# Last norm on token rows with the residual added by TensorE, other skipped splits, and the root spread inside a unit

## What is computed

```python
def layer_norm(x, g, b):
    xf = x.astype(jnp.float32)
    mu = xf.mean(-1, keepdims=True)
    var = jnp.mean(jnp.square(xf - mu), -1, keepdims=True)
    return ((xf - mu) * lax.rsqrt(var + LN_EPS) * g.astype(jnp.float32) + b.astype(jnp.float32)).astype(x.dtype)
```

## Time and profile before

| | before |
|---|---|
| median of 3 runs | 928.47 us (927.08 to 929.01) |
| the profiled execution | 931.21 us |
| its span | 929.4 us |
| TensorE matmul busy | 895.8 us |
| VectorE busy | 679.0 us |
| ScalarE busy | 505.5 us |
| GpSimd busy | 125.5 us |
| granted TensorE clock, mean | 0.99 of full |
| read from HBM | 153.97 MB |

### The profile page before, as it was taken

How to read it: one execution, slowest core, us unless ns; L and a number is a source line. 1 busy time by engine, 2 the same in 40 slices (tenths; PEclk the granted TensorE clock), 3 DMA queues, 4 the chain that set the end, 5 groups by cost and what they waited for, 6 DMA issues and landing times.

```text
span 929.4 us, 18682 instructions
## 1 busy us (share of the span) xinstructions
PE 895.8 (96%) x7034; PEld 859.4 (92%) x7034; DVE 679.0 (73%) x1123; ACT 505.5 (54%) x753; POOL 125.5 (13%) x80
## 2 busy tenths in 40 slices
PE   6999799999999999999999999999999899999995
PEld 5977799999999999899999999999889899999995
DVE  5976787777777847778766776878676776667667
ACT  6345644433435556876555555564486654455453
POOL 1000000000000023001232310301210122223011
PEclk9999999999999999999999999999999999999998
DMA  8953275556553654336555555532324255556531
GB/s 306 334 205 100 90 226 182 180 181 198 179 188 121 220 185 159 133 114 219 184 173 192 168 193 182 182 114 92 113 93 162 82 187 181 180 181 191 177 106 46
DMA packets 44004, 155.71 MB, mean 168 GB/s; under 512 B 5066, under 2 KB 5557, under 8 KB 43957
## 3 DMA queue, kind: packets, MB, share of 16 engines
q1 hardware_dynamic: 42192, 151.12, 49.2%
q10 hardware_dynamic: 1317, 2.35, 0.7%
q0 software_dynamic: 448, 1.59, 0.6%
HBM read 153.97 MB, written 1.06 MB: 167 GB/s over the span
## 4 chain that ended last, share of the span: by engine, by line
PE 86%; DVE 5%; ACT 4%; issue 3%; POOL 1%; DMA 1%; SPq 0%; POOLq 0%; ACTq 0%; DVEq 0%
PE ps L394 21%; PE ps L395 21%; PE ps L396 21%; PE ps L438 3%; PE ps L440 3%; PE ps L439 3%; PE ps L411 1%; PE ps L418 1%; PE ps L412 1%; DVE w_lo L1277 1%; PE ps L483 1%; PE ps L485 1%; PE ps L484 1%; PE ps L501 1%; PE ps L764 1%
## 5 line engine op out<-in xcount | busy, mean ns | idle before, releaser
L394 PE MATMUL ps<-op_hi,w_hi 128*128 128x258 f32 (+1 forms) x1372 | 390.3, 284 | 0.9 <-DVE op_lo L1406 0.9
L396 PE MATMUL ps<-op_hi,w_lo 128*128 128x258 f32 (+1 forms) x1372 | 387.6, 283 | 0.0
L395 PE MATMUL ps<-op_lo,w_hi 128*128 128x258 f32 (+1 forms) x1372 | 387.4, 282 | 0.0
L1277 DVE TENSOR_TENSOR w_lo<-raw,w_hi 128x1024 fp32r<-128x1024 f32 x224 | 283.0, 1282 | 28.9 <-ACT w_hi L928 27.5
L928 ACT ACTIVATE w_hi<-raw 128x1024 fp32r<-128x1024 f32 x224 | 231.4, 1051 | 62.8 <-PE ps L396 30.6
L394 PEld LDWEIGHTS ps<-op_hi,w_hi 128*128 128x128 f32 x1372 | 260.1, 190 | 3.7 <-issue 1.6
L395 PEld LDWEIGHTS ps<-op_lo,w_hi 128*128 128x128 f32 x1372 | 260.9, 190 | 1.1
L396 PEld LDWEIGHTS ps<-op_hi,w_lo 128*128 128x128 f32 x1372 | 260.0, 189 | 0.0
L394 PE MATMUL ps<-mix_hi,w_hi 128*128 128x256 f32 x480 | 137.7, 287 | 2.5 <-DVE w_lo L1274 2.3
L396 PE MATMUL ps<-mix_hi,w_lo 128*128 128x256 f32 x480 | 135.7, 283 | 0.0
L395 PE MATMUL ps<-mix_lo,w_hi 128*128 128x256 f32 x480 | 135.7, 283 | 0.0
(11 more groups left out here) (251 smaller groups left out, 1091.2 us busy)
## 6 DMA issues: line engine op xcount, KB each, us to landing
raw<-in_stream SPq DMA_DIRECT2D x284, 512.0 KB, 3.4
x<-in_x SPq DMA_DIRECT2D x4, 256.0 KB, 5.6
bias<-bias_rows POOLq DMA_DIRECT2D x1, 1024.0 KB, 7.9
result<-x SPq DMA_DIRECT2D x4, 256.0 KB, 2.4
spans<-in_spans ACTq DMA_DIRECT2D x1, 576.0 KB
bias<-bias_rows POOLq DMA_DIRECT2D x1, 512.0 KB, 11.2
proj<-in_gmask ACTq DMA_DIRECT2D x1, 512.0 KB
masks<-in_masks ACTq DMA_DIRECT2D x1, 384.0 KB
```

The source lines that it names most:

```text
L394: pe.matmul(o, wh, xh, start=start, stop=False, **kw)
L395: pe.matmul(o, wh, xl, start=False, stop=False, **kw)
L396: return pe.matmul(o, wl, xh, start=False, stop=stop, **kw)
L1277: m = dve.tensor_tensor(w_lo[:, s, :], raw[:, s, :], fp(w_hi[:, s, :]), ALU.subtract)
```

## The change

1. In all feed-forwards, TensorE does the spread of the root after half of its third unit (`out_chunk` with `half`), not behind the unit. On VectorE only one split is left between the statistic and the copy of the root; the second stands behind the first hidden chunk, as does the small operation on the FFN variance (L1500 before).
2. In the last feed-forward the first two splits are made; the last four are left out.
3. In the last feed-forward the down products are `row_chunk`, tokens on partitions. The last two are cut by token half (`row_part`), and between them 16 fp32 matmuls add ALPHA times `x`, with `x` as the stationary operand and a scaled identity (`alpha_ident`) as the moving one.
4. The last norm is made on token rows: squares with their sums on ScalarE straight from the banks, gain and shift as rows loaded by a new 1 MB DMA, root as a scalar for each partition, result stored as rows.

```diff
-            for i in range(4):
-                sp.dma_start(pair(out, i), pair(x, i)).then_inc(S["out_stored"], 16)
+            sp.dma_start(last_norm, d["last_norm"]).then_inc(S["last_loaded"], 16)
+            for i in range(4):
+                t, n = i // 2, slice(i % 2 * 512, i % 2 * 512 + 512)
+                sp.dma_start(out[t, :, n], result[:, t, n]).then_inc(S["out_stored"], 16)
...
-            inverse_root(7)
+            row_roots(2)
...
+            def row_part(ahead, xh, xl, t, last=False):
+                pe.wait_ge(S["split_done"], unit.at(ahead + 1))
+                s, tok = (unit.n + ahead) % SLOTS, slice(t * P, t * P + P)
+                for f in range(2):
+                    n = slice(f * 512, f * 512 + 512)
+                    pe.matmul(bank(2 * t + f), xh[:, tok], w_hi[:, s, n], start=False, stop=False, skip_group_check=True)
+                    pe.matmul(bank(2 * t + f), xh[:, tok], w_lo[:, s, n], start=False, stop=False, skip_group_check=True)
+                    m = pe.matmul(bank(2 * t + f), xl[:, tok], w_hi[:, s, n], start=False, stop=last, skip_group_check=True)
+                    if last and t + f < 2:
+                        m.then_inc(S["acc_done"], 1)
...
+            def add_residual():
+                for c in range(NCH):
+                    if c % 2 == 0:
+                        pe.wait_ge(S["x_centred"], 12 + c // 2 + 1)
+                    for t in range(2):
+                        pe.matmul(ps[:, 2 * t + c // 4, c % 4 * P:c % 4 * P + P], x[:, c, t * P:t * P + P], alpha_ident[:],
+                                  start=False, stop=False, skip_group_check=True)
...
-                out_chunk(bank(6, 0, n), hi, lo)
+                out_chunk(bank(6, 0, n), hi, lo, half=0)
                 spread([(0, 0, SEQ), (1, 0, SEQ + P)])
+                out_chunk(bank(6, 0, n), hi, lo, half=1)
...
-                down(0, j + NFF - 1)
-                down(1, j + NFF, last=True)
+                if final:
+                    pe.wait_ge(S["h_ready"], j + NFF - 1)
+                    row_part(0, h_hi[:, 0, :], h_lo[:, 0, :], 0)
+                    pe.wait_ge(S["alpha_ready"], 1)
+                    add_residual()
+                    pe.wait_ge(S["h_ready"], j + NFF)
+                    row_part(1, h_hi[:, 1, :], h_lo[:, 1, :], 0, last=True)
+                    row_part(0, h_hi[:, 0, :], h_lo[:, 0, :], 1)
+                    row_part(1, h_hi[:, 1, :], h_lo[:, 1, :], 1, last=True)
...
-                        step(ahead=not skip[0])
-                        skip[0] -= skip[0] > 0
+                        step(ahead=not (late and isinstance(j, int) and j == NFF - 1))
...
+            act.activation(alpha_ident[:], ident[:], ACT.Copy, scale=ALPHA).then_inc(S["alpha_ready"], 1)
...
+            for b in range(4):
+                acc_complete(b)
+                act.activation(wide[:, b * 512:b * 512 + 512], bank(b), ACT.Square, scale=D ** -0.5,
+                               accum_out=row_sq[:, b:b + 1]).then_inc(S["row_sq_ready"], 1)
...
+            def last_layer_norm(n):
+                def variance(t):
+                    dve.wait_ge(S["row_sq_ready"], 4 * n + 2 * t + 2)
+                    dve.tensor_scalar(row_var[:, t:t + 1], row_sq[:, 2 * t:2 * t + 1], row_sq[:, 2 * t + 1:2 * t + 2],
+                                      LN_EPS, ALU.add, ALU.add).then_inc(S["row_var_ready"], 1)
+                def gain(t, f):
+                    dve.wait_ge(S["row_sq_ready"], 4 * n + 2 * t + f + 1)
+                    own.done(dve.tensor_tensor(piece(gained, t, f), bank(2 * t + f), last_norm[:, 0, f * 512:f * 512 + 512],
+                                               ALU.mult))
+                def finish(t, f):
+                    dve.wait_ge(S["row_root_ready"], 2 * n + t + 1)
+                    dve.scalar_tensor_tensor(piece(result, t, f), piece(gained, t, f), row_root[:, t:t + 1],
+                                             last_norm[:, 1, f * 512:f * 512 + 512], ALU.mult, ALU.add
+                                             ).then_inc(S["result_ready"], 1)
...
+                        hand_statistic(0, eps)
+                        step()
+                        copy_rinv(0)
...
+                    if begins:
+                        split_lo()
```

More of the change, by code:

```diff
@@ L535, in down @@
                     pe.wait_ge(S["h_ready"], j)
-                    (in_chunk if shifted else row_chunk)(h_hi[:, c, :], h_lo[:, c, :], first, last)
+                    (in_chunk if shifted and not final else row_chunk)(h_hi[:, c, :], h_lo[:, c, :], first, last)
                 j = hidden.n
@@ L1365, in post_norm, with piece @@
                     sum_squares(1)
-            def layer_norm(gain, shift, layer, final=False):
+            def last_layer_norm(n):
+                def piece(v, t, f):
+                    return v[:, t, f * 512:f * 512 + 512]
+                def variance(t):
[11 more added lines that the diff above has]
+                                             ).then_inc(S["result_ready"], 1)
+                dve.wait_ge(S["last_loaded"], 16)
+                gain(0, 0)
+                variance(0)
+                gain(0, 1)
+                own.settle()
+                finish(0, 0)
+                finish(0, 1)
+                gain(1, 0)
+                variance(1)
+                gain(1, 1)
+                own.settle()
+                finish(1, 0)
+                finish(1, 1)
@@ L1369, in layer_norm @@
+            def layer_norm(gain, shift, layer):
                 k = ln.n
                 ln.n += 1
[L1371 to L1375 removed]
+                dve.wait_ge(S["shift_hi"], k + 1)
+                own.done(dve.tensor_tensor(op_lo_wide[:, :, SEQ:],
+                                           vcol(shift, layer * 8, 8).unsqueeze(2).to_broadcast([P, NCH, 2]),
+                                           fp(op_hi_wide[:, :, SEQ:]), ALU.subtract))
@@ L1380, in layer_norm @@
                                              ).then_inc(S["z_ready"], 1)
-                if final:
-                    sum_squares(0)
-                    sum_squares(1)
-                    hand_statistic(7, LN_EPS)
-                    for c in range(NCH):
-                        own.done(dve.tensor_scalar(y[:, c, :], y[:, c, :], vcol(gain, layer * 8 + c), None, ALU.mult))
-                    own.settle()
-                    dve.wait_ge(S["spread_done"], stats.n)
-                    for i in range(4):
-                        dve.tensor_tensor(pair(sq, i), pair(y, i), over(chunk(7, 1), 2), ALU.mult
-                                          ).then_inc(S["scaled"], 1)
-                    return
                 def rest(c):
@@ L1493, in _ @@
             rinvs = [0]
-            def operand_scale(eps, skip, convolve):
-                hand_statistic(0, eps)
-                if convolve:
-                    dve.wait_ge(S["var_ready"], stats.n)
-                    own.done(dve.tensor_scalar(tok_ffn[:], tok_var[:, 0:2], eps, None, ALU.mult))
-                for part in range(2):
-                    step(ahead=not skip[0])
-                    skip[0] -= skip[0] > 0
-                copy_rinv(0)
             def split_p():
@@ L1982 @@
          for n, a in arrays.items()}
-    out = nc.dram_tensor("result", (P, NCH, SEQ), F32, kind="ExternalOutput").ap()
+    out = nc.dram_tensor("result", (2, P, D), F32, kind="ExternalOutput").ap()
     build(nc, d, out)
```

61 lines of the change are left out of this document (31 added, 30 removed).

## The result

The changed kernel took 923.25 us in the median of 8 runs (922.79 to 924.70), the kernel before 928.74 in the median of 8 (926.73 to 931.61). Runs of both on one chip give a ratio of 0.9929, with a 95% interval of 0.9912 to 0.9945: **0.7% faster**, 0.5 to 0.9%. The profiled executions are 931.21 and 923.63 us, their spans 929.4 and 921.8. Medians here are over undisturbed executions; two of the later ones, of 1465.5 and 1250.6 us at a granted clock of 0.56 and 0.66, are left out.

What follows compares the result with a forecast made beforehand. The prediction took TensorE, busy 895.8 of 929.4 us, to bound the kernel. Its terms, 0.8 - 0.6 + 3.2 + 1.2 + 2.4 = 7.0 us, came off the median 928.47 to give 921.5, range 918.8 to 925.6.

Steps and rivals of the forecast that it cites:

- first start: Start of the first feed-forward: earlier spread brings the hidden chunk sooner, 0.8 us gained (bounds 0.5 and 1.4).
- second start: Start of the second feed-forward: a new wait on the power ahead of the spread, 0.6 us lost (bounds 0 and 0.8).
- third start, "skipped splits": Start of the last feed-forward: weights split early, 1.7 us of wait and 1.5 of clock, 3.2 gained.
- rows: Down products on token rows, last feed-forward: 0.06 us for each of 20 units, 1.2 gained (bounds 0 and 1.6).
- tail: From the last two down products to the end: end at 926.95 against 929.4, 2.4 us gained (bounds 0.8 and 3.2).
- The power is held up: All three feed-forward starts: VectorE's split stretches GpSimd's power to 1.7 us, so each spread waits about 0.6.
- the rival with 0.7: Feed-forward starts: the power is not held up, three waits of 0.6 us go, 1.9 more gained, 919.6; chance 15%.
- Step 5: Last norm: VectorE's own queue, not ScalarE, makes the second variance late; last finishing operations end at 924.15.
- The residual: Between the last two down products: 16 fp32 matmuls at 0.23 us, 3.7 in all, on top of TensorE's work.
- the slower rival: Residual: none of 32 weight loads overlap, 14.9 us instead of 3.7, total 932.7; chance 3%.
- the rival in which it does: Feed-forward starts: the clock falls at three new waits of 0.6 us, 1.5 lost apiece, total 926.0; chance 4%.
- The rival with "less clock to win": Third start and tail: half-speed stretch missing in other runs, 1.5 less; tail at low bound, 1.6 less; 924.6; chance 15%.

Runs made afterwards that it cites:

- whole_unit: The changed kernel with the root's spread behind the whole unit again: 922.88 us, ratio 0.9913 to the kernel before.
- power_first: The changed kernel, but VectorE waits for GpSimd's power before its split: 920.77 us, ratio 0.9897 to the kernel before; run again 920.00 us.
- by_unit: The changed kernel with the last two down products ordered by unit, then by token half: 924.55 us in one run.
- changed_again: The changed kernel with no further edit, timed again on one chip: 923.49 us, ratio 0.9921 to the kernel before.

## Why the prediction was right

It said 921.5, with a range of 918.8 to 925.6, and faster with a chance of 0.92. The median is 923.25, 1.75 over it and inside. Direction and size are well hit; single terms miss by up to 1.0. The sum of 7.0 has to be compared with the profiled executions, 7.6, since it was worked out in one; the medians differ by 5.5. By its own steps:

| term | forecast | measured | where |
|---|---|---|---|
| first start | 0.8 | 0.75 | first FF; 0.76 in whole_unit |
| second start | -0.6 | -0.40 | second FF; -0.40 in whole_unit |
| third start, "skipped splits" | 3.2 | 3.70 | third FF less the rows; 0.3 of it at the other end |
| rows | 1.2 | 0.80 | two pairs of profiles, 0.80 and 0.82 |
| tail | 2.4 | 3.38 | 6.74 - 3.36 |
| earlier than the first mark | 0 | -0.64 | same code |
| sum | 7.0 | 7.6 | |

That the sum is nearer than its parts is luck: 0.4 too much for the rows and 0.64 lost ahead of the first mark stand against 1.0 too little for the tail and 0.5 for the third start.

- **The power is held up.** All three took 1.61 to 1.68 as forecast; the rival with 0.7 is wrong, and power_first shows the cause. The wait was sized at 0.6, and from start to start the spreads are 0.57 to 0.61 late. The second stretch lost only 0.40 because the prediction read no hole at its first down product, where 0.29 stood to be won.
- **The third start.** Its two parts are right: the product starts 1.78 us sooner in its stretch (735.22 - 691.44 = 43.78 against 736.72 - 691.16 = 45.56; forecast 1.7), and the next one follows it after 8.56 instead of 10.17, which is 1.61 for the clock and the restart (forecast 1.5). The remaining 0.3 came at the other end, where the prediction noted two splits less beside GpSimd's centring and put no price on them. **The step that failed** is the sentence that credits both parts to the skipped splits. I wrote that the spread brings the hidden chunk 0.8 sooner, "the same order of operations as the second has", and left out that on ScalarE the split stood behind an operation that waits for the root, so that the spread moves the split forward too. Alone, that shrinks the hole to 0.89, and the clock held in both profiles that have it. In this kernel the edit that I priced at 3.2 is worth 0.72, 0.3 of that at the other end, and the two together are worth 0.3 less than the better one alone.
- **Rows: over-sized by 0.4.** 0.04 for each unit instead of 0.06, which was the difference of two single units; over 15 chunks it is 0.045. By the fixed 2.5 ns a matmul of the Trainium skill ("TensorE: Matmul & The Clock Gate", section Back-to-back issue gap) it would have been an estimated 0.6 in all; the measured 0.8 decides. That estimate came nearer than my 1.2.
- **The tail was mis-sized by 1.0.** TensorE needs 8.93 where I had 9.1 (920.15 - 911.08), since the residual's matmuls go at 3.48 / 16 = 0.2175, not 0.23. From the last matmul to the last operation's end it is 3.60 (919.39 - 915.79), not 4.0. The last store takes 2.41 (921.8 - 919.39), not the 2.8 of the earlier trace rows. That store differs in what was issued close before it, and no run here varied that, so the reason for the 0.4 is open.
- **Step 5, VectorE's queue and not ScalarE.** Only just so. The last sum is there at 916.90 (916.71 + 0.19), the gain that VectorE works at until then ends at 917.10 and the variance starts at 917.02: the two are level. by_unit shows the mechanism where it does bind, 1.5 us.
- **The residual** has the forecast size, and its loads overlap (0.2175 for each matmul); the slower rival (14.9 us) is wrong by a wide margin. "TensorE has this on top" was too strict: 0.76 of it fills a wait.
- **The clock did not fall at the new waits**; the rival in which it does was rightly held unlikely.
- **1.75 over the forecast.** The profiled execution before is 2.5 above its median, that after 0.4. The rival with "less clock to win" said so. It was half right at most: the tail kept its full gain. How much the clock moves the time is on record. In the 38 executions of the kernel before that were timed beside the experiments, the span goes with the mean granted clock: 928.7 to 931.4 us at 0.990 (20 of them), 926.9 to 927.5 at 0.994 (10), 924.8 to 925.1 at 0.996 (3). The profiled one, 929.4 at 0.990, is of the first kind. A mean of 0.996 leaves some 3.7 us lost to the clock (0.004 x 925), and the profile loses some 4 in the windows from 920 to its end alone. So, as an estimate, those three had no half-speed stretch in the third start, and there the change has about 1.6 less to win. On the chip of changed_again, where 8 of 11 executions before stood at 0.990, the medians were 931.06 and 923.49, 7.6 apart. Which stretch was slow in an execution that was only timed is not on record.

## What to carry to other kernels

When a short GpSimd operation lies on the path that TensorE waits for, don't let a long VectorE operation with two inputs start ahead of it: a wait of 0.8 us on VectorE made it 2.4 times as fast, and paid at three places. When two edits touch the same hole, price them together, and measure each alone as well as taken out: here they were worth 3.99 and 2.98 alone and 3.70 together; taking the skipped splits out of the pair cost 0.72, taking the spread out of it gained 0.31. To tell a wait's whole cost, count from start to start of the matmuls: a bracket of 0.45 stood for 0.7. Follow a moved operation through its engine's queue to everything behind it, not only to the result it was moved for.

## What the runs showed of the hardware that was not expected

**The same code takes one of two times.** Stretches A and B of the tables are the same in all eleven profiles. A took 30.43 to 30.51 in nine of them and 28.92 or 28.94 in two. B took 52.63 to 52.71 in seven and 51.11 or 51.15 in four. Nothing lies between. The kernel before, then power_first, in B:

```profile
632.74 1.11 PE L764 MATMUL ps<-proj 64*128 64x64 f32 x16 [1.22 <-DVE proj L1700]
...
636.73 0.42 PE L395 MATMUL ps<-op_lo,w_hi 128*128 128x258 f32 x1
```

```profile
631.56 1.11 PE L806 MATMUL ps<-proj 64*128 64x64 f32 x16 [1.23 <-DVE proj L1753]
...
634.08 0.29 PE L401 MATMUL ps<-op_lo,w_hi 128*128 128x258 f32 x1
```

The same wait stands ahead of the same work, 1.22 and 1.23, and behind it a matmul of 258 columns takes 0.42 us in one and 0.29 in the other. The windows from 636 to 638 give the clock:

```profile
636.00:638.00 2.00, 2.00 (x12) 2.00 (x11) 1.33 (x2) 1.01 (x2) 0.00 (x0) 0.58 0.28 113
```

```profile
636.00:638.00 2.00, 2.00 (x25) 1.80 (x24) 1.86 (x4) 0.00 (x0) 0.00 (x0) 1.00 0.19 27
```

That is mostly 1.2 GHz in the first and 2.4 GHz in the second, without any edit there. Power_first, traced twice, has A slow and B fast the one time, A fast and B slow the other. So a time of this kernel carries steps of 1.5 us of chance, as large as most terms here. That they make most of the scatter of the times is likely: in the 38 executions above the span goes with the mean granted clock. Where the clock fell in them is not shown.

**How long a wait may be** has no clean answer here. Behind 2.34 us the clock was 0.50, but in one profile, and the same chance may have had a part in it: then the 1.6 that the third start got back in clock is not there in every execution, as the estimate above has it. Behind 1.43, 0.89 and the new 0.4 it stayed at 1.00 where I looked, and behind 1.22 it did either.
